# First mixer of a two-block transformer kernel: eight of twelve modulation blocks summed on GpSimd instead of TensorE

## The chip, the cores and the metric

One Trainium2 chip, one of its cores. The metric is the device time of one execution in microseconds (us), the median of the runs that are shown.

## What is computed

Two blocks, one after the other, on 256 tokens of width 1024 in fp32. The first block starts from a vector `c` of 1024 numbers that sets shifts, scales and gates:

```python
mod = jax.nn.silu(c) @ w_ada[l] + b_ada[l]                       # w_ada: 1024 x 6144
shift1, scale1, gate1, shift2, scale2, gate2 = jnp.split(mod, 6, axis=-1)
h = modulate(rms_norm(x, norm1_g[l]), shift1, scale1)
proj = h @ w_in[l]                                               # 1024 x 5120
q_sb, k_sb, v_sb, q_mb, k_mb, v_mb, g_sb, g_mb = jnp.split(proj, cuts, axis=-1)
o_sb, o_mb = stick_breaking_attention(...), moba_attention(...)
merged = sigmoid(g_sb) * (o_sb @ w_branch_sb[l]) + sigmoid(g_mb) * (o_mb @ w_branch_mb[l])
x = x + gate1[:, None, :] * (merged @ w_out[l])
h2 = modulate(rms_norm(x, norm2_g[l]), shift2, scale2)
y = moe_ffn(h2, ...)                                             # 64 experts, top 8
x = x + gate2[:, None, :] * y
```

The second block has a convolution, a low-rank attention, a cross attention to a memory and a second mixture of 16 experts. The change touches only `silu(c) @ w_ada`, which is cut into twelve blocks of 512 columns, called ada0 to ada11.

## The kernel before

The kernel is one program with an instruction list written by hand for each engine. All weights of the first mixer come through a ring of six places of 2 MB (`ring`, places of 128 partitions x 4096 fp32). `CHUNKS_A` (line 152) is the order in which SyncE (SP) loads them, all through line 581. A chunk of `w_in`, `w_branch` or `w_out` is split into two parts: ScalarE writes the rounded high part into the next place of the ring (`high`, line 799, four quarters of 128x1024), VectorE writes the rest over the chunk (`low_part`, line 1178, four quarters), and TensorE multiplies three times, high by high, high by low, low by high. Such a chunk takes two slots (`slots_of`, line 172), a modulation block takes one, as `WHOLE` says. Slot m lies in place m mod 6, and the chunk of slot m may be loaded when slot m-6 is given back: SP (line 595) and ScalarE before it writes a high part (line 793) wait for the count `used_a`, which TensorE raises at its first product behind the last use of a slot, or once that last use is done.

A modulation block on TensorE has two parts. `modulation(n, ...)` (line 2112) makes eight products of 128x32 with 512 columns, silu(c) against the block, into a bank of PSUM; ScalarE copies the bank to SBUF (`ada_copy`, the helper at line 776). `columns(n - 1)` (line 2100) then makes four products with one column each, which turn the row of 512 numbers into four columns of bank 7. `mod_full` counts these. VectorE waits for ten of them at line 1325, before it merges the two branches.

The order on TensorE: ada0 to ada3; in0, in1, in2, ada4, in3, in4, ada5, in5 (each in chunk about 11 us); then four steps p = 0 to 3, one for each pair of heads:

```python
zz{p}, ss{p}            # scores, lines 2219 to 2230
project in{6+p}_0       # line 2016; columns(5 + p); attend(p - 1), line 2211
half of in{6+p}_1       # line 2024
wait sb_rest; skip{p}   # lines 2243 to 2245
wait at_p_ready; pT{p}  # lines 2250 to 2252
half of in{6+p}_1; modulation(6 + p)
```

`sb_rest` comes from VectorE's line 1300, `at_p_ready` from its line 1306, behind the lines 1277 to 1305 of the same step. VectorE then makes quarters 0 and 1 of the low part of chunk 7+p, line 1318, and quarters 2 and 3, which the next step's in chunk needs. Behind the four steps come the branches (line 2268: three quarters of brs_0, `columns(9)`, attend(3), three of brs_1, then brm_0 and the rest), out0 to out3 (line 2016), the sums of squares (line 2059), ada10 and ada11 (`modulation` at lines 2302 and 2303), logit1 (line 2309) and the routing. `columns(10)` and `columns(11)` run in gate2, during the routing.

Behind the first mixer, the experts of the first mixture stream through the same ring: four fixed ones first, then those that the routing table names. GpSimd (POOL) does nothing but four constants at the start.

## Time and profile before

| | |
|---|---|
| median of 3 runs | 1531.04 us (1530.39 to 1534.06) |
| the profiled execution | 1528.67 us |
| its span, first to last instruction | 1526.9 us |
| first mixer up to logit1 | 0 to 247 us |
| routing | 247 to 269 us |
| first mixture of experts | 269 to 757 us |
| second mixer | 757 to 1086 us |
| second mixture of experts | 1086 to 1514 us |
| TensorE busy | 87% of the span |
| GpSimd busy | 0.2 us |

Busy time is counted for compute instructions. Start times are microseconds from the start of the span. "idle before" is the time that the engine stood still ahead of a group, with what released it behind the arrow.

### The profile page before, as it was taken

Reading aid. Unit: us, or ns where it says so; the run is one execution under the profiler, and the core shown is the slowest. Engines: PE = TensorE matmul, PEld = TensorE weight load, DVE = VectorE, ACT = ScalarE, POOL = GpSimd, SP = SyncE. Lnnn points to the kernel's source line nnn. Section 1 sums busy time; section 2 is a strip of 40 time slices with the busy share of each in tenths; the row PEclk is TensorE's granted clock in tenths of the full one; section 3 lists DMA queues with packets and bytes.
Section 4 is the critical chain, followed back from the end, with each engine's and each line's share of the span. In section 5 each row is a group of like instructions: output and inputs, shape, how many; then the busy total and the mean of one; then the engine's idle time right before and its main releaser. Section 6 shows DMA issues by size and latency. Waiting matters only on the chain.

```text
span 1526.9 us, 26211 instructions
## 1 busy us (share of the span) xinstructions
PE 1321.8 (87%) x11250; PEld 935.0 (61%) x11250; DVE 540.3 (35%) x1185; ACT 405.9 (27%) x630; POOL 0.2 (0%) x4
## 2 busy tenths in 40 slices
PE   6999998999999999999799999999876567566656
PEld 3888897666766765565588999999623213223222
DVE  3546665434233222322474775753301001001001
ACT  3557743111111111111264346452201000000001
POOL 0000000000000000000000000000000000000000
PEclk9999999999999999999999999999989869779787
DMA  9864659799999999999933344747999999999995
GB/s 398 304 267 169 275 208 393 307 408 388 425 423 422 428 424 424 424 421 420 409 129 143 139 161 166 279 165 296 391 427 428 427 428 429 428 428 428 429 428 231
DMA packets 46365, 523.58 MB, mean 343 GB/s; under 512 B 5273, under 2 KB 6841, under 8 KB 8761
## 3 DMA queue, kind: packets, MB, share of 16 engines
q1 hardware_dynamic: 44784, 519.16, 82.3%
q10 hardware_dynamic: 1480, 2.96, 0.6%
q8 instruction: 78, 1.28, 0.3%
q14 instruction: 23, 0.18, 0.0%
HBM read 520.85 MB, written 1.24 MB: 342 GB/s over the span
## 4 chain that ended last, share of the span: by engine, by line
PE 63%; DMA 31%; DVE 3%; ACT 1%; issue 1%; SPq 0%; ACTq 0%; DVEq 0%
PE psum L2016 17%; DMA arena<-in_w_exp_up_dram 14%; PE psum L2480 10%; DMA arena<-in_w_exp_down_dram 9%; PE psum L2580 5%; DMA ring<-in_w_gate_up_e_dram 4%; PE psum L2413 3%; PE psum L2996 3%; PE psum L2402 3%; DMA ring<-in_w_down_e_dram 2%; PE psum L2024 2%; PE psum L2268 2%; PE psum L2030 1%; PE psum L2835 1%; PE psum L2451 1%; DMA ring<-in_w_ada_dram 1%
## 5 line engine op out<-in xcount | busy, mean ns | idle before, releaser
L2016 PE MATMUL psum<-arena_r,ring_r 128*128 128x256 f32 x2176 | 272.5, 281 | 3.5 <-DVE arena_r L1185 3.1
L2016 PEld LDWEIGHTS psum<-arena_r,ring_r 128*128 128x128 f32 x2176 | 261.3, 188 | 8.7 <-issue 4.9
L2480 PE MATMUL psum<-ring,arena 128*32 128x256 f32 (+1 forms) x2304 | 184.2, 391 | 10.0 <-DMA ring<-in_w_gate_up_e_dram 9.3
L1178 DVE TENSOR_TENSOR ring_r<-ring,ring_r 128x1024 fp32r<-128x1024 f32 x140 | 163.0, 1219 | 59.9 <-ACT ring_r L799 59.2
L2480 PEld LDWEIGHTS psum<-ring,arena 128*32 128x32 f32 (+1 forms) x2304 | 111.1, 123 | 75.2 <-issue 16.5
L2996 PE MATMUL psum<-ring,arena 128*32 128x256 f32 x1408 | 103.2, 448 | 52.2 <-DMA ring<-in_w_exp_gate_dram 28.3
L799 ACT ACTIVATE ring_r<-ring 128x1024 fp32r<-128x1024 f32 x140 | 137.4, 1050 | 18.3 <-DMA ring<-in_w_out_dram 5.2
L2996 PEld LDWEIGHTS psum<-ring,arena 128*32 128x32 f32 x1408 | 48.8, 125 | 99.6 <-DMA ring<-in_w_exp_gate_dram 32.3
L3013 PE MATMUL psum<-ring,arena 128*32 128x512 f32 x384 | 67.2, 835 | 41.3 <-DMA ring<-in_w_exp_down_dram 37.5
L1951 DVE TENSOR_TENSOR arena<-arena,psum 128x256 f32<-128x256 f32 x16 | 6.7, 422 | 237.0 <-ACT arena L1137 237.0
L2580 PE MATMUL psum<-ring,arena 128*32 128x512 f32 (+1 forms) x544 | 87.6, 597 | 2.7 <-DMA ring<-in_w_down_e_dram 1.8
L1134 ACT ACTIVATE arena<-psum 128x512 f32<-128x512 f32 x16 | 9.6, 597 | 257.4 <-PE psum L2996 257.4
L776 ACT ACTIVATE arena<-psum 128x512 f32<-128x512 f32 (+3 forms) x76 | 43.6, 580 | 125.0 <-PE psum L2746 27.4
L3013 PEld LDWEIGHTS psum<-ring,arena 128*32 128x32 f32 x384 | 12.2, 132 | 91.6 <-DMA ring<-in_w_exp_down_dram 63.9
L2996 PE MATMUL psum<-arena 128*32 128x256 f32 x576 | 44.6, 466 | 26.9 <-DMA arena<-in_w_exp_up_dram 26.9
L938 ACT ACTIVATE arena<-psum 128x512 f32<-128x512 f32 x25 | 14.9, 598 | 195.3 <-PE psum L2480 195.3
L1586 DVE SCALAR_TENSOR_TENSOR arena_r<-psum,small,arena_r 128x512 fp32r<-128x512 f32 x25 | 18.8, 750 | 134.8 <-ACT arena_r L960 134.8
L2402 PE MATMUL psum<-arena_r 128*128 128x256 f32 x400 | 61.3, 291 | 3.2 <-DVE arena_r L1590 3.2
L1561 DVE COPY arena<-psum 128x384 f32<-128x384 f32 (+1 forms) x60 | 35.1, 585 | 78.5 <-PE psum L2413 76.8
L2402 PEld LDWEIGHTS psum<-arena_r 128*128 128x128 f32 x400 | 52.8, 190 | 10.8 <-issue 5.8
L2413 PE MATMUL psum<-arena_r 128*128 128x384 f32 (+1 forms) x304 | 55.7, 323 | 0.8 <-DVE arena_r L1467 0.8
L2580 PEld LDWEIGHTS psum<-ring,arena 128*32 128x32 f32 (+1 forms) x544 | 24.4, 120 | 52.2 <-issue 49.3
(425 smaller groups left out, 1524.4 us busy)
## 6 DMA issues: line engine op xcount, KB each, us to landing
ring<-in_w_gate_up_e_dram SPq DMA_DIRECT2D x56, 2048.0 KB, 16.8
ring<-in_w_down_e_dram SPq DMA_DIRECT2D x60, 1024.0 KB, 14.9
ring<-in_w_exp_gate_dram SPq DMA_DIRECT2D x29, 2048.0 KB, 35.2
ring<-in_w_exp_down_dram SPq DMA_DIRECT2D x24, 2048.0 KB, 35.8
ring<-in_w_in_dram SPq DMA_DIRECT2D x20, 2048.0 KB, 8.7
ring<-in_w_exp_up_dram SPq DMA_DIRECT2D x15, 2048.0 KB, 35.7
arena<-in_w_exp_up_dram SPq DMA_DIRECT2D x15, 2048.0 KB, 36.2
ring<-in_w_ada_dram SPq DMA_DIRECT2D x12, 2048.0 KB, 12.5
```

The lines of the kernel that those rows point to most:

```text
L776: frees(A(dst, src, ACT.Copy), name)
L799: A(hi, whole, ACT.Copy).then_inc(w_high, 1)
L1178: V.tensor_tensor(lo, whole, hi.bitcast(F32), ALU.subtract).then_inc(w_low, 1)
L1561: V.tensor_copy(dst, src).then_inc(g_copied, 1)
L2016: ins = product(lambda a_, b_, k, first, last: mm(ps[:, t * T:(t + 1) * T], a_[:, k, c], b_[:, k, :], start=first, stop=last), w, x, None ...
L2024: return product(lambda a_, b_, k, first, last: mm(ps[:, t * T:(t + 1) * T], a_[:, k, c], b_[:, k, :], start=first, stop=last, skip_group_ ...
L2402: ins = mm(acc(m), y[:, m * P:(m + 1) * P], PT1[j], start=(opens and m % 2 == 0 and y is y_hi), stop=False, skip_group_check=True)
L2413: ins = mm(psum[:, 4 + 3 * (n % 2), k * width:(k + 1) * width], h[:, t, kk * P:(kk + 1) * P], Pg1[:, t, c0:c0 + width], start=(t == 0 and ...
L2480: ins = mm(psum[c, 5, 256 * r:256 * r + 256], xg1[:, k, P * j + width * e:P * j + width * (e + 1)], w[:, k, :], start=(k == 0), stop=(k == ...
L2580: ins = mm(psum[width * b:width * (b + 1), 4 + 3 * half, :], hidden(b, e, k), dn[e][:, k, half * 512:(half + 1) * 512], start=(k == 0), st ...
L2996: ins = mm(psum[32 * q:32 * q + 32, b, g], xg[:, kk, CAP2 * e:CAP2 * (e + 1)], w[k][:, 256 * q:256 * (q + 1)], start=(kk == 0), stop=(kk = ...
L3013: ins = mm(psum[32 * e:32 * e + 32, 5 + 2 * half, :], aT2[e][:, k, :], w(e)[:, half * 512:(half + 1) * 512], start=(k == 0), stop=(k == KT ...
```

## The change

The eight products of ada4 to ada11 leave TensorE, and ScalarE's eight copies go with them. GpSimd gets a program of its own: when a block has landed, it multiplies each of its eight 128x512 parts by the number of silu(c) that belongs to the partition, in place, then adds halves (2048 columns, then 1024, then 512) until one row of 512 per partition is left. TensorE's four one-column products now sum over all 128 partitions, with ones in place of the selecting column. Each of the three adds waits for the one before it, the last one also for `mod_full`.

The blocks move in the ring's order: ada6 to ada9 one place of the order ahead, and ada10 and ada11 from behind `w_out` to behind in9. The slots of the eight blocks are given back by GpSimd (`mod_rows`), all others by TensorE (`used_a`). `columns(4)` stands behind in4, `columns(5)` to `columns(9)` where they stood. The load of `w_up_sh` moves behind the four fixed experts.

```diff
-ADA_BEHIND = {2: (4,), 4: (5,), 6: (6,), 7: (7,), 8: (8,), 9: (9,)}
-ADA_PAIR = 6
+ADA_BEHIND = {2: (4,), 4: (5,), 5: (6,), 6: (7,), 7: (8,), 8: (9,), 9: (10, 11)}
...
-CHUNKS_A += [("w_branch_sb", 0, 1024, 4), ("w_branch_mb", 0, 1024, 4), ("w_out", 0, 512, 8), ("w_out", 512, 512, 8),
-             ("w_ada", 512 * (ADA - 2), 512, 8), ("w_ada", 512 * (ADA - 1), 512, 8)]
+CHUNKS_A += [("w_branch_sb", 0, 1024, 4), ("w_branch_mb", 0, 1024, 4), ("w_out", 0, 512, 8), ("w_out", 512, 512, 8)]
...
-NU = NA
+GP_SLOTS = [SLOT_A[IN_ADA[_j]] for _j in range(ADA_FIRST, ADA)]
+NU = NA - len(GP_SLOTS)
...
-        csil = buf(6, 8, 256)
+        csil = mod[:, 40:48]
...
+        summed_rows = ada_rows + [buf(12, 512, 512 * _i) for _i in (1, 2, 3, 1, 2, 3)]
...
+        def given_back(eng, m):
+
+            if m in GP_SLOTS:
+                eng.wait_ge(mod_rows, GP_SLOTS.index(m) + 1)
+            else:
+                eng.wait_ge(used_a, sum(s not in GP_SLOTS for s in range(m + 1)))
...
-                    sp.wait_ge(used_a, SLOT_A[n] - RING + 1)
+                    given_back(sp, SLOT_A[n] - RING)
...
-            sp.wait_ge(mod_full, ADA - 2)
-            sp.dma_start(up_sh, a["w_up_sh"].rearrange("p (k f) -> p k f", k=KT)).then_inc(up_sh_in, 16)
             pair(0, (E1 - 4, E1 - 3))
             pair(3, (E1 - 2, E1 - 1))
+            full(sp, "gate2")
+            sp.dma_start(up_sh, a["w_up_sh"].rearrange("p (k f) -> p k f", k=KT)).then_inc(up_sh_in, 16)
...
-                for n in ADA_BEHIND.get(c, ()):
-                    ada_copy(n)
...
-                if p:
-                    ada_copy(ADA_PAIR - 1 + p)
...
-            copy_out("ada10", late_rows[0])
-            copy_out("ada11", late_rows[1])
...
+        @block.gpsimd
+        def _(gp):
+            G = nc.gpsimd
+            gp.wait_ge(csil_ready, 1)
+            steps = 0
+            for n in range(ADA_FIRST, ADA):
+                arrived(gp, ("a", IN_ADA[n]))
+                w = ring[:, SLOT_A[IN_ADA[n]] % RING, :].rearrange("p (k c) -> p k c", k=KT)
+                for k in range(KT):
+                    ins = G.tensor_scalar(w[:, k, :], w[:, k, :], csil[:, k:k + 1], None, ALU.mult)
+                ins.then_inc(gp_step, 1)
+                for half in (4, 2):
+                    steps += 1
+                    gp.wait_ge(gp_step, steps)
+                    G.tensor_tensor(w[:, 0:half, :], w[:, 0:half, :], w[:, half:2 * half, :], ALU.add).then_inc(gp_step, 1)
+                steps += 1
+                gp.wait_ge(gp_step, steps)
+                gp.wait_ge(mod_full, n - 1 if n < ADA_FIRST + 2 else n - 2)
+                if n == ADA_FIRST + 2:
+                    full(gp, "ms0")
+                G.tensor_tensor(summed_rows[n - ADA_FIRST], w[:, 0, :], w[:, 1, :], ALU.add).then_inc(mod_rows, 1)
...
-                evacuated(pe, f"ada{n}")
+                if n < ADA_FIRST:
+                    evacuated(pe, f"ada{n}")
+                    rows, over = ada_rows[n % 2], sel_col
+                else:
+                    pe.wait_ge(mod_rows, n - ADA_FIRST + 1)
+                    rows, over = summed_rows[n - ADA_FIRST], ones[:, 0:1]
...
-                for i, n in enumerate(ADA_BEHIND.get(c, ())):
-                    modulation(n, IN_A[c] + 1 + i, held)
-                    held = None
+                if c == 4:
+                    pe.wait_ge(mod_ready, 2)
+                    columns(ADA_FIRST).then_inc(mod_full, 1)
...
                     if p and i == 0:
-                        ins.then_inc(used_a, 1)
+                        ins.then_inc(used_a, 2)
...
-                modulation(ADA_PAIR + p, IN_A[6 + p] + 1, (used_a, 2))
...
-            modulation(ADA - 2, n0 + 14)
-            modulation(ADA - 1, n0 + 15, gives=(used_a, 1))
```

Three places show how the instructions move. SP's loads in the first mixer, from in5 on, in the kernel before (every load waits for TensorE's count):

```order
L581 DMA ring<-in_w_in_dram 128x4096 [waits chunks_used_a] x2
L581 DMA ring<-in_w_ada_dram 128x4096 [waits chunks_used_a]
L581 DMA ring<-in_w_in_dram 128x4096 [waits chunks_used_a]
L581 DMA ring<-in_w_ada_dram 128x4096 [waits chunks_used_a]
L581 DMA ring<-in_w_in_dram 128x4096 [waits chunks_used_a]
```

The same stretch of SP's loads in the changed kernel:

```order
L590 DMA ring<-in_w_in_dram 128x4096 [waits modulation_rows_summed]
L590 DMA ring<-in_w_ada_dram 128x4096 [waits chunks_used_a]
L590 DMA ring<-in_w_in_dram 128x4096 [waits chunks_used_a]
L590 DMA ring<-in_w_ada_dram 128x4096 [waits modulation_rows_summed]
L590 DMA ring<-in_w_in_dram 128x4096 [waits chunks_used_a]
L590 DMA ring<-in_w_ada_dram 128x4096 [waits modulation_rows_summed]
```

Every modulation block but two, in5 and out0 now stand behind GpSimd's count; in5 waits for ada4, ada7 for ada5, and so on.

TensorE from the end of one pair step into the next, in the kernel before (L2024 is the last half of the in chunk, L2112 the modulation, L2219 the next scores):

```order
L2024 MATMUL psum<-arena_r,ring_r 128x256 x24
L2112 MATMUL psum<-ring,items 32x512 x8
L2219 MATMUL psum<-arena 128x256 x2
L2223 MATMUL psum<-arena 128x128 x2
L2228 MATMUL psum<-arena 128x128 x2
L2230 MATMUL psum<-arena 128x256 x2
L2016 MATMUL psum<-arena_r,ring_r 128x256 x48
```

and in the changed kernel:

```order
L2052 MATMUL psum<-arena_r,ring_r 128x256 x24
L2237 MATMUL psum<-arena 128x256 x2
L2241 MATMUL psum<-arena 128x128 x2
L2246 MATMUL psum<-arena 128x128 x2
L2248 MATMUL psum<-arena 128x256 x2
L2044 MATMUL psum<-arena_r,ring_r 128x256 x48
```

The eight products between two steps are gone; the in chunk follows sooner on the step before.

GpSimd's list for one block in the changed kernel (it stands there eight times):

```order
L1172 TENSOR_SCALAR ring<-ring,mod 128x512 x8
L1177 TENSOR_TENSOR ring<-ring 128x2048
L1177 TENSOR_TENSOR ring<-ring 128x1024
L1183 TENSOR_TENSOR arena<-ring 128x512
```

Before, GpSimd had no such instruction.

## Rows read from the trace of the kernel before

**Rows 1.** The page: busy time of each engine.

```profile
PE 1321.8 (87%) x11250; PEld 935.0 (61%) x11250; DVE 540.3 (35%) x1185; ACT 405.9 (27%) x630; POOL 0.2 (0%) x4
```

**Rows 2.** Windows: length, busy PE, PEld, DVE, ACT, POOL, granted clock, DMA share, GB/s.

```profile
108.00:190.00 82.00, 80.13 (x686) 69.93 (x685) 55.16 (x81) 59.72 (x94) 0.00 (x0) 1.00 0.56 221
450.00:550.00 100.00, 98.73 (x812) 67.58 (x812) 31.59 (x96) 13.19 (x22) 0.00 (x0) 1.00 1.01 423
```

**Rows 3.** Timeline of TensorE: start, length, line, instructions, idle before.

```profile
68.41 1.92 PE L2112 MATMUL psum<-ring,items 128*32 128x512 f32 x16
70.77 11.44 PE L2016 MATMUL psum<-arena_r,ring_r 128*128 128x256 f32 x96 [0.44 <-PE psum L2112]
...
111.79 5.88 PE L2016 MATMUL psum<-arena_r,ring_r 128*128 128x256 f32 x48
...
126.51 1.92 PE L2112 MATMUL psum<-ring,items 128*32 128x512 f32 x16
128.36 0.70 PE L2219 MATMUL psum<-arena 64*128 64x256 f32 x4
...
188.03 2.37 PE L2268 MATMUL psum<-arena_r,ring_r 128*128 128x256 f32 x18 [0.78 <-ACT arena L776]
...
192.56 20.75 PE L2268 MATMUL psum<-arena_r,ring_r 128*128 128x256 f32 x174
```

**Rows 4.** Timeline of all engines from ada10 to the first logits.

```profile
242.03 3.64 PE L2112 MATMUL psum<-ring,items 128*32 128x512 f32 x32
246.53 3.30 ACT L913 ACTIVATE arena<-arena,mod 128x256 f32<-128x256 f32 x8 [1.74 <-DVE arena L1214]
247.19 3.34 PE L2309 MATMUL psum<-arena 128*64 128x256 f32 x16 [1.52 <-ACT arena L913]
```

**Rows 5.** Windows around a stretch in which TensorE stands still.

```profile
757.00:759.00 2.00, 0.16 (x2) 0.15 (x2) 1.93 (x4) 2.00 (x4) 0.00 (x0) 1.00 1.00 426
761.00:763.00 2.00, 2.00 (x12) 2.00 (x11) 2.00 (x5) 1.52 (x3) 0.00 (x0) 0.50 0.64 239
```

**Rows 6.** DMA, 160 to 216 us: the branch loads, median us from issue to landing.

```profile
ring<-in_w_branch_sb_dram SPq DMA_DIRECT2D x1, 2048.0 KB, 7.5
ring<-in_w_branch_mb_dram SPq DMA_DIRECT2D x1, 2048.0 KB, 12.4
```

**Rows 7.** Groups of VectorE by form, 46 to 200 us: busy us, mean ns.

```profile
L1178 DVE TENSOR_TENSOR ring_r<-ring,ring_r 128x1024 fp32r<-128x1024 f32 x40 | 46.8, 1221 | 26.2 <-ACT ring_r L799 26.1
L1306 DVE TENSOR_SCALAR arena<-arena,small 128x256 f32<-128x256 f32 x8 | 2.8, 346 | 0.0
L1285 DVE SCALAR_TENSOR_TENSOR arena<-psum,arena 128x512 f32<-128x512 f32 x4 | 2.7, 680 | 0.0
L1305 DVE TENSOR_SCALAR arena<-arena,small 128x128 f32<-128x128 f32 x8 | 2.3, 283 | 0.1
```

**Rows 8.** Timeline of SP and ScalarE: the load of ada4, the high part of out0.

```profile
46.23 0.33 SPq L581 DMA_DIRECT2D ring<-in_w_ada_dram  x1
...
203.67 3.90 ACT L799 ACTIVATE ring_r<-ring 128x1024 fp32r<-128x1024 f32 x4 [3.28 <-DVE arena L1338]
```

**Rows 9.** One pair step (p = 1) on VectorE and TensorE, in order of time.

```profile
136.09 0.69 DVE L1300 TENSOR_TENSOR arena<-arena,constants 128x512 f32<-128x512 f32 x1
138.09 0.34 DVE L1306 TENSOR_SCALAR arena<-arena,small 128x256 f32<-128x256 f32 x1
140.81 0.59 PE L2243 MATMUL psum<-arena,constants 128*128 128x256 f32 x2
142.56 0.27 PE L2250 MATMUL psum<-constants,arena 128*128 128x128 f32 x1
145.27 2.36 DVE L1178 TENSOR_TENSOR ring_r<-ring,ring_r 128x1024 fp32r<-128x1024 f32 x2 [1.55 <-ACT ring_r L799]
149.48 5.87 PE L2016 MATMUL psum<-arena_r,ring_r 128*128 128x256 f32 x48
```

**Rows 10.** VectorE ahead of the first pair step.

```profile
101.12 3.26 DVE L1255 SCALAR_TENSOR_TENSOR arena<-arena,vectors 128x256 f32<-128x256 f32 x8 [5.61 <-ACT arena L823]
```

More of the change, by code:

```diff
@@ L199 @@
 for _c in range(6):
-    JOBS += [f"in{_c}_{_j}" for _j in range(2)] + {3: ["ms0"], 4: ["sum0"]}.get(_c, []) + [f"ada{_j}" for _j in ADA_BEHIND.get(_c, ())]
+    JOBS += [f"in{_c}_{_j}" for _j in range(2)] + {3: ["ms0"], 4: ["sum0"]}.get(_c, [])
 for _p in range(PAIRS):
-    JOBS += [f"zz{_p}", f"ss{_p}", f"in{6 + _p}_0"] + ([f"av{_p - 1}"] if _p else []) + [f"in{6 + _p}_1", f"skip{_p}", f"pT{_p}", f"ada{ADA_PAIR + _p}"]
+    JOBS += [f"zz{_p}", f"ss{_p}", f"in{6 + _p}_0"] + ([f"av{_p - 1}"] if _p else []) + [f"in{6 + _p}_1", f"skip{_p}", f"pT{_p}"]
 JOBS += ["brs_0", f"av{PAIRS - 1}", "brs_1", "brm_0", "brm_1", "brs_2", "brm_2", "brs_3", "brm_3"]
-JOBS += ["out0", "out1", "out2", "ms2", "out3", "ada10", "ada11", "logit1"]
+JOBS += ["out0", "out1", "out2", "ms2", "out3", "logit1"]
 JOBS += ["hN0", "route1", "hN1", "hN2", "hN3", "gate2", "shg", "rank1", "count1", "tabT", "start1", "itemR", "itemW", "eidx"]
@@ L230 @@
         continue
-    while (_name == "logit1" and _next % BANKS != 6) or (_name == "cq" and _next % BANKS != 4) or (_name == "ms7" and _next % BANKS <= 3):
+    while (_name == "brs_2" and _next % BANKS != 2) or (_name == "logit1" and _next % BANKS != 6) or (_name == "cq" and _next % BANKS != 4) or (_name == "ms7" and _next % BANKS <= 3):
         _next += 1
@@ L2092, in idle_products, with columns, modulation @@
                     mm(ps[:, 0:T], ones, cst[:, 0:T], start=True, stop=True)
-            def columns(n, place=None, rows=None, gives=None):
-                evacuated(pe, f"ada{n}")
+            def columns(n, place=None):
+                if n < ADA_FIRST:
+                    evacuated(pe, f"ada{n}")
+                    rows, over = ada_rows[n % 2], sel_col
+                else:
+                    pe.wait_ge(mod_rows, n - ADA_FIRST + 1)
+                    rows, over = summed_rows[n - ADA_FIRST], ones[:, 0:1]
                 place = psum[:, 7, 4 * ADA_ORDER[n]:4 * ADA_ORDER[n] + 4] if place is None else place
-                rows = (pair_rows if n >= ADA_PAIR else ada_rows)[n % 2] if rows is None else rows
                 for b in range(4):
-                    ins = mm(place[:, b:b + 1], rows[:, b * P:(b + 1) * P], sel_col, start=True, stop=True)
-                    if gives is not None and b == 0:
-                        ins.then_inc(*gives)
+                    ins = mm(place[:, b:b + 1], rows[:, b * P:(b + 1) * P], over, start=True, stop=True)
                 return ins
-            def modulation(n, place, gives=None):
+            def modulation(n, place):
                 w = chunk_a(place, 512)
@@ L2113, in modulation @@
                                  start=(k == 0), stop=(k == 1))
[L2114 to L2115 removed]
                 done(ins, f"ada{n}")
[L2117 to L2126 removed]
+                full(pe, f"ada{n}")
+                used(used_a, 1)
             def norm_sums(name, sqb, ready):
@@ L2146, in _ @@
             columns(ADA_FIRST - 1).then_inc(mod_full, 1)
-            n0 = IN_A[9] - 8
             def project_by_halves(w):
@@ L2273, in branch @@
                     done(ins, name)
-            ws = chunk("a", n0 + 10, whole=False)
-            branch("brs_0", ws, 0, 0, range(3), SPLIT_AT[("a", n0 + 10)], gives=(used_a, 1))
+            ws = chunk("a", IN_BRANCH["s"], whole=False)
+            branch("brs_0", ws, 0, 0, range(3), SPLIT_AT[("a", IN_BRANCH["s"])], gives=(used_a, 2))
             columns(ADA - 3).then_inc(mod_full, 1)
@@ L2279, in _ @@
             branch("brs_1", ws, 0, 2, range(3))
-            wm = chunk("a", n0 + 11, whole=False)
+            wm = chunk("a", IN_BRANCH["m"], whole=False)
             evacuated(pe, f"skip{PAIRS - 1}")
-            branch("brm_0", wm, 4, 0, range(3), SPLIT_AT[("a", n0 + 11)])
-            branch("brs_0", ws, 0, 0, (3,), SPLIT_AT[("a", n0 + 10)])
-            branch("brm_0", wm, 4, 0, (3,), SPLIT_AT[("a", n0 + 11)])
+            branch("brm_0", wm, 4, 0, range(3), SPLIT_AT[("a", IN_BRANCH["m"])])
+            branch("brs_0", ws, 0, 0, (3,), SPLIT_AT[("a", IN_BRANCH["s"])])
+            branch("brm_0", wm, 4, 0, (3,), SPLIT_AT[("a", IN_BRANCH["m"])])
             branch("brs_1", ws, 0, 2, (3,))
```

37 lines of the change are left out of this document (15 added, 22 removed).

## The prediction

> **What bounds the kernel now.** I read the page first: TensorE is busy 87% of the span, VectorE 35%, ScalarE 27%, and GpSimd 0.2 us [rows 1]. The windows then tell the stages apart [rows 2]. In the first mixer TensorE works 80.1 of 82 us, while the DMA engines have a share of 0.56: TensorE bounds, and what leaves its list there is time, unless something else is late. Around 450 to 550 us the DMA share is 1.01 and TensorE is busy 98.7 of 100: the experts run at the speed of the loads. But those loads start when TensorE gives ring places back, so an earlier mixer starts that stretch earlier by as much, and a later one later. I carry every microsecond of the mixer to the end one for one.
>
> **What the change takes away.** The timeline of TensorE prices it [rows 3]. From the start of ada4 to the start of in3 it is 70.77 - 68.41 = 2.36 us. ada5 to ada9 each cost the distance from their start to the next work, 128.36 - 126.51 = 1.85 us; five make 9.25 us. The wait of 0.78 us ahead of 188.03 is for ScalarE's copy of ada9 and goes with it. Together 12.4 us. The one-column products stay. ada10 and ada11 are 3.64 us, yet worth nothing: from 242 us on ScalarE and VectorE make the norm and the modulated input, and TensorE's logits start at 247.19, released by ScalarE, 1.5 us after ada11 is over [rows 4]. Without them TensorE stands still for those 5 us. Elsewhere a stop has cost clock: from 757 to 759 TensorE worked 0.16 us, the granted clock was still 1.00, and in 761 to 763 it was 0.50, which is 1.2 of 2.4 GHz [rows 5]. The logits and transposes behind the gap could run at that level for some of the routing. They are half paced by ScalarE, so I put this at 1 us, bounds 0 and 3.
>
> ScalarE's eight copies, off the path, cost nothing and give nothing. w_up_sh goes behind the fixed experts, whose loads gain the place of ada10 and ada11: nothing either way, since the share in the mixer leaves room [rows 2].
>
> **What the new order of the ring costs.** w_branch_mb was loaded into the place of ada8, which came back at the start of the last pair step, and took 12.4 us to land beside w_branch_sb, which took 7.5 [rows 6]. Now it needs in9's place, which comes back only at the first product of brs_0. That product moves from 188.03 to about 175.6. The load lands 7.5 us after it, at 183.5 with the issue; one quarter on ScalarE (3.90 us for four) and one on VectorE (1.22) [rows 7, 8] make the first quarter ready at 185.9, the others follow at 1.2 us each, and the fourth, behind the copy of av3 on ScalarE, at about 189.7. TensorE wants it earlier: in the timeline brm_0 starts 18 products of 0.119 us after 192.56, at 194.7 [rows 3], so at 182.3 now. It ends its first pass some 5.6 us late. This cost doesn't depend on GpSimd.
>
> Up to here: -12.4 + 5.6 + 1 = **-5.8 us**.
>
> **What GpSimd costs.** No row shows a GpSimd instruction of this kind; the nearest are VectorE's [rows 7]. From 283 ns for 128 columns and 346 for 256, both from SBUF to SBUF, a product of 512 is about 0.47 us on VectorE, 0.49 ns a column. The plain pace is that of 680 ns for 512 and 1221 for 1024, 1.06 ns a column. The adds of 2048, 1024 and 512 come to 2.3, 1.22 and 0.68 by it. So a block is 8 x 0.47 + 4.2 = 8.0 us if GpSimd has VectorE's best pace, and 2 x (8 x 0.68 + 4.2) = 19.3 at half its plain one. I take 12 us, nearer to the plain pace (9.6) because these are the same operations; 11 instructions, 1.09 us in the mean. That alone is hidden: ada4, issued at 46.23, has landed by about 57; the eighth sum must be there for the high part of out0, at 203.67 before and some 7 us sooner now [rows 8], and 139 us over eight is 17.4 us a block.
>
> What is not hidden is the company of VectorE. The two prices of a product above (0.49 ns a column against 1.06) show that VectorE draws on a second path to SBUF where it can. I assume that this path is GpSimd's too, and that an instruction of VectorE which wants it waits for the GpSimd instruction in progress. No row of this trace speaks for or against, for GpSimd never runs beside VectorE here. The Trainium skill, SBUF — State Buffer, section "Who interferes with whom", states it outright: a VectorE instruction with two SBUF inputs contends with a GpSimd instruction that reads SBUF, and the one that comes second blocks until the first is done. By that page the sum is the one that follows, without it -5.8.
>
> With 12 us of work in a step that shrinks to 17.8 us, GpSimd is busy 0.67 of the time, and a VectorE instruction loses 0.67 x 1.09 = 0.73 us. In a pair step there are eleven of them: lines 1292, 1296, 1300, four of 1305 and 1306, four of 1178.
> - Up to the skip products three lose 2.2 us. Line 1300 ended at 136.78, TensorE came at 140.81: 4.0 us of slack [rows 9]. Nothing.
> - Up to pT seven lose 5.1 us, slack 142.56 - 138.43 = 4.1: **1.0 us**.
> - The last two quarters of the next chunk's low part ended at 147.63, and TensorE wanted them at 149.48. These 1.85 us are just what the missing modulation takes away, so their delay of 1.5 us counts in full: **1.5 us**.
>
> 2.5 us in each of three steps is 7.5. Ahead of the first step stand eight of line 1255 and the four quarters of in6. The eight start at 101.12 [rows 10], now 4.2 us earlier at 97, and take 1.14 each instead of 0.41: to 106.1. Four quarters at 1.95 bring it to 113.9, where TensorE wants them at 111.79 - 4.2 = 107.6 [rows 3]: 6.3 us. Two quarters in the branches: 1.5 us. Sum 15.3, net of -5.8: **+9.5 us**.
>
> With 8 us a block the same working gives 0.33 us an instruction, 5 us in all, net -1. With 16 us it gives 1.3 us each: 7.7 a step, 13.4 ahead of them, 2.6 in the branches, 39 in all, net +33. Against the profiled execution of 1528.67 us this is 1538.2, and since the median of the runs shown lies 2.4 us above it, 1540.6 us; the forecast's own range is 1530 to 1565.
>
> The Trainium skill has the one price of GpSimd that I know: GPSIMD Engine Reference, section 3.1, gives 4497 ns for an add of 2048 columns against 2293 on VectorE. By it the adds take 8.3 us instead of the 6 or so in my 12, a block some 14, and the sum would be about +20.
>
> **Rivals.**
> 1. *The two engines don't meet.* The splits run at 1.22 us as before, GpSimd is hidden below 17.4 us a block, and what is left is -5.8: 1525.2 us, faster. For it speaks that nothing in the trace shows a shared path; against it the second path that the product prices show. It decides as soon as the delay of a VectorE instruction is under about 0.35 us, where the stalls fall below 5.8. Chance 0.34, of which 0.25 is faster by over 0.3% (4.6 us, about what a measurement of this kernel can tell from no change) and 0.09 within.
> 2. *GpSimd is simply too slow.* Beyond 17.4 us a block the eighth sum is late for out0, whatever VectorE does; at 19.3 it comes 8 x 1.9 = 15 us late, net +9, and the blocks behind it in the ring (in5 behind ada4, in7 behind ada7) begin to drag: 1540 to 1560. Chance 0.10.
> 3. *They meet, but GpSimd gives way.* VectorE's eleven instructions are some 8.5 us of a step, which leaves GpSimd 9.3 for its 12: it falls 2.7 us behind in each of four steps and a few more in the projections, well inside the 8 x 5.4 us that it has to spare. VectorE then waits only at the first instruction of a row, for the rest of what GpSimd has begun, in all 3 to 8 us: 1528 to 1533. Chance 0.10: 0.03 faster, 0.05 within, 0.02 slower.
>
> The forecast has the other 0.46: 0.39 slower by over 0.3%, 0.07 within. Sums: 0.28 faster, 0.21 within 0.3%, 0.51 slower. The range reaches from rival 1 with its bounds, 1523, to the forecast with 16 us a block, 1566.
>
> **What would show it.** In the profile of the changed kernel: line 1178's successor stays at 1.22 us in the mean if rival 1 holds, or is well above it; the GpSimd rows sum to 12 us a block, or over 17. TensorE idles ahead of the in chunks of the pair steps, released by VectorE's low part, in the forecast, and nowhere but at brm_0 in rival 1. An idle stretch of about 5 us ahead of logit1 with a lower granted clock behind it, and w_branch_mb issued at the first product of brs_0, belong to every case. I am wrong at the root if the mixer changes by one amount and the whole by another, that is, if the experts don't pass the shift on.

## The result, and the profile after

The changed kernel takes 1585.18 us (median of 4 runs, 1583.62 to 1585.81), the kernel before 1530.72 us in the runs beside it (4 runs, 1526.07 to 1534.06): a ratio of 1.0359, 95% interval 1.0342 to 1.0376. Slower by 54.5 us, where I had forecast 9.5, and 19 us past the end of my range. The profiled execution has a span of 1584.0 us against 1526.9 before.

The page of the changed kernel, busy time of each engine and the first row of the chain that ended last:

```profile
PE 1322.8 (84%) x11122; PEld 948.3 (60%) x11122; DVE 577.5 (36%) x1185; ACT 401.5 (25%) x622; POOL 200.1 (13%) x92
...
PE 50%; DMA 30%; POOL 13%; DVE 4%; ACT 2%; issue 1%; SPq 0%; POOLq 0%; ACTq 0%; DVEq 0%
```

TensorE has lost its 128 products (11250 before) and is no less busy: its mean granted clock over the span is 0.923, against 0.941 before. The first version below, with the same 11122 products and hardly any work on GpSimd, is busy 1307.4 us; so some 15 us of TensorE's busy time go to the lower clock behind its waits, and belong to the delay. GpSimd is new with 200.1 us, and it stands in the chain with 13% of the span, about as much. I had 96 us in mind for it (8 x 12). Its groups by form (busy us, mean ns, idle before):

```profile
L1172 POOL TENSOR_SCALAR ring<-ring,mod 128x512 f32<-128x512 f32 x64 | 125.5, 1977 | 54.9 <-DMA ring<-in_w_ada_dram 54.9
L1177 POOL TENSOR_TENSOR ring<-ring 128x2048 f32<-128x2048 f32 x8 | 37.7, 4711 | 0.7
L1177 POOL TENSOR_TENSOR ring<-ring 128x1024 f32<-128x1024 f32 x8 | 22.9, 2856 | 0.6
L1183 POOL TENSOR_TENSOR arena<-ring 128x512 f32<-128x512 f32 x8 | 14.0, 1751 | 0.6
```

A product takes 1977 ns in the mean, where I had 0.68 us as the dearer bound by VectorE's rows [rows 7]. How much of that is GpSimd's own shows in the last block of its timeline, since VectorE has no instruction between 235.3 and 258.3 us (start, us, line, instructions):

```profile
208.66 18.57 POOL L1172 TENSOR_SCALAR ring<-ring,mod 128x512 f32<-128x512 f32 x8
227.31 7.44 POOL L1177 TENSOR_TENSOR ring<-ring 128x2048 f32<-128x2048 f32 x2
234.83 1.61 POOL L1183 TENSOR_TENSOR arena<-ring 128x512 f32<-128x512 f32 x1
236.43 12.34 POOL L1172 TENSOR_SCALAR ring<-ring,mod 128x512 f32<-128x512 f32 x8
248.85 6.91 POOL L1177 TENSOR_TENSOR ring<-ring 128x2048 f32<-128x2048 f32 x2
255.83 1.26 POOL L1183 TENSOR_TENSOR arena<-ring 128x512 f32<-128x512 f32 x1
```

The last block takes 257.09 - 236.43 = 20.7 us by itself: eight products of 1.54 us, adds of 6.91 together and 1.26. The one before it took 27.8. The eight blocks run back to back from 55.27 to 257.09 us, 25.2 us each: behind its first product GpSimd stands still for 1.9 us in all (the last column above, where 54.9 us lie ahead of that product). So no load, no ring place and no other engine sets the end of the eighth sum, but GpSimd's own pace. My sum had 12, and my upper bound was 19.3.

Who waits for that? The waits of ScalarE and of SP's queue between 50 and 320 us (waited for: us, times, longest):

```profile
ACT ring_r L811 <- POOL arena L1183: 38.5, 2, 27.7
```

```profile
SPq L590 <- POOL arena L1183: 122.3, 6, 25.6
```

SP waits six times, 122.3 us, for a place that GpSimd holds, and ScalarE waits 27.7 us for the eighth sum, which must be there before the high part of out0 is written (line 799 before, 811 now). TensorE on its side, same columns:

```profile
PE psum L2044 <- DVE arena_r L1213: 23.8, 2, 20.9
PE psum L2044 <- DVE ring_r L1206: 8.6, 4, 4.4
PE psum L2237 <- DVE arena L1346: 8.3, 3, 4.4
PE psum L2285 <- DVE ring_r L1206: 7.0, 2, 5.8
```

The timeline of TensorE says where: these are the starts that answer to rows 3 and 4, with the idle time before them in brackets.

```profile
211.34 1.94 PE L2285 MATMUL psum<-arena_r,ring_r 128*128 128x256 f32 x6 [5.78 <-DVE ring_r L1206]
...
263.79 2.90 PE L2044 MATMUL psum<-arena_r,ring_r 128*128 128x256 f32 x12 [20.89 <-DVE arena_r L1213]
269.56 17.84 PE L2044 MATMUL psum<-arena_r,ring_r 128*128 128x256 f32 x132 [2.87 <-DVE arena_r L1213]
...
302.64 2.79 PE L2324 MATMUL psum<-arena 128*64 128x256 f32 x11 [5.09 <-ACT arena L921]
```

| start of | before, us | after, us | later by |
|---|---|---|---|
| first pair step | 110.28 | 108.74 | -1.5 |
| second pair step | 128.36 | 133.26 | 4.9 |
| fourth pair step | 167.57 | 182.05 | 14.5 |
| brs_0 | 188.03 | 211.34 | 23.3 |
| out0 | 213.15 | 263.79 | 50.6 |
| logit1 | 247.19 | 302.64 | 55.5 |

From logit1 to the end it is 1281.4 us now and 1279.7 before: the experts pass the shift on, as predicted. Everything happens before logit1, so **the start of logit1 is the measure** in what follows, beside the time. It serves for versions that leave work out too, as nothing before it depends on the values, while the routing behind it does.

Each version has one trace, and the traces differ before GpSimd has anything to do. The load of ada4, issued at 46.23 us in the kernel before [rows 8], is issued here in the change and in the version with short adds below:

```profile
47.06 0.33 SPq L590 DMA_DIRECT2D ring<-in_w_ada_dram  x1
```

```profile
50.65 0.33 SPq L590 DMA_DIRECT2D ring<-in_w_ada_dram  x1
```

The versions spread from 46.03 to 50.83 us, and none of this is GpSimd's work, which starts some 8 us later. Where a few microseconds decide, I therefore count the start of logit1 **from that issue**: 200.96 us before, 255.58 us in the change, 54.6 later, as the time is.

VectorE was held as well, and the row shows it plainly. The eight instructions of line 1283 (line 1255 before, [rows 10]) read and write SBUF:

```profile
98.07 11.23 DVE L1283 SCALAR_TENSOR_TENSOR arena<-arena,vectors 128x256 f32<-128x256 f32 x8 [2.27 <-ACT arena L835]
```

3.26 us before, 11.23 now. The splits of line 1206 (line 1178 before) take 1781 ns in the mean between 46 and 260 us, against 1221 [rows 7], the longest 5.6 us. So two suspects remain: GpSimd's own chain of blocks, and VectorE blocked by GpSimd.

### The profile page after: what moved, and what is told of

Read it like the earlier page. It is cut to its first block, busy times and chain, and to the rows that moved or that the text cites. A ratio compares the mean times of both kernels' runs of the same rounds, so it can differ in the third digit from the quotient of the medians.

```text
span 1584.0 us, 26036 instructions
## 1 busy us (share of the span) xinstructions
PE 1322.8 (84%) x11122; PEld 948.3 (60%) x11122; DVE 577.5 (36%) x1185; ACT 401.5 (25%) x622; POOL 200.1 (13%) x92
## 3 DMA queue, kind: packets, MB, share of 16 engines
q10 hardware_dynamic: 1480, 2.96, 0.6%
q8 instruction: 77, 1.26, 0.3%
## 4 chain that ended last, share of the span: by engine, by line
PE 50%; DMA 30%; POOL 13%; DVE 4%; ACT 2%; issue 1%; SPq 0%; POOLq 0%; ACTq 0%; DVEq 0%
DMA arena<-in_w_exp_up_dram 14%; PE psum L2044 13%; DMA arena<-in_w_exp_down_dram 9%; PE psum L2495 9%; POOL ring L1172 8%; PE psum L2595 5%; DMA ring<-in_w_gate_up_e_dram 4%; POOL ring L1177 4%; PE psum L2428 3%; PE psum L3011 3%; PE psum L2417 2%; DMA ring<-in_w_down_e_dram 2%; PE psum L2850 1%; PE psum L2466 1%; PE psum L2182 1%; PE psum L2464 1%
## 5 line engine op out<-in xcount | busy, mean ns | idle before, releaser
L2044 PE MATMUL psum<-arena_r,ring_r 128*128 128x256 f32 x2176 | 283.4, 287 | 34.0 <-DVE arena_r L1213 25.3
L2044 PEld LDWEIGHTS psum<-arena_r,ring_r 128*128 128x128 f32 x2176 | 272.0, 195 | 39.7 <-issue 23.6
L1206 DVE TENSOR_TENSOR ring_r<-ring,ring_r 128x1024 fp32r<-128x1024 f32 x140 | 186.7, 1388 | 102.1 <-ACT ring_r L811 100.8
L811 ACT ACTIVATE ring_r<-ring 128x1024 fp32r<-128x1024 f32 x140 | 137.5, 1050 | 77.0 <-POOL arena L1183 38.5
L2495 PEld LDWEIGHTS psum<-ring,arena 128*32 128x32 f32 (+1 forms) x2304 | 109.7, 121 | 71.9 <-issue 13.4
L1172 POOL TENSOR_SCALAR ring<-ring,mod 128x512 f32<-128x512 f32 x64 | 125.5, 1977 | 54.9 <-DMA ring<-in_w_ada_dram 54.9
L788 ACT ACTIVATE arena<-psum 128x512 f32<-128x512 f32 (+3 forms) x68 | 38.6, 577 | 105.3 <-PE psum L2761 27.4
L1177 POOL TENSOR_TENSOR ring<-ring 128x2048 f32<-128x2048 f32 (+1 forms) x16 | 60.5, 3784 | 1.3
```

The source lines that it names most:

```text
L788: frees(A(dst, src, ACT.Copy), name)
L811: A(hi, whole, ACT.Copy).then_inc(w_high, 1)
L1172: ins = G.tensor_scalar(w[:, k, :], w[:, k, :], csil[:, k:k + 1], None, ALU.mult)
L1177: G.tensor_tensor(w[:, 0:half, :], w[:, 0:half, :], w[:, half:2 * half, :], ALU.add).then_inc(gp_step, 1)
L1206: V.tensor_tensor(lo, whole, hi.bitcast(F32), ALU.subtract).then_inc(w_low, 1)
L2044: ins = product(lambda a_, b_, k, first, last: mm(ps[:, t * T:(t + 1) * T], a_[:, k, c], b_[:, k, :], start=first, stop=last), w, x, None ...
```

## The experiments

Theory A: the chain. Eight blocks one behind the other end too late for the ring and for out0. Theory B: the company. VectorE's low parts are late because GpSimd's instructions hold it. The first four kernels ran before any of them was known.

**The work left out.** The change with only the last add of each block:

```diff
-                for k in range(KT):
-                    ins = G.tensor_scalar(w[:, k, :], w[:, k, :], csil[:, k:k + 1], None, ALU.mult)
-                ins.then_inc(gp_step, 1)
-                for half in (4, 2):
-                    steps += 1
-                    gp.wait_ge(gp_step, steps)
-                    G.tensor_tensor(w[:, 0:half, :], w[:, 0:half, :], w[:, half:2 * half, :], ALU.add).then_inc(gp_step, 1)
...
```

> The changed kernel with GpSimd's eight products and first two adds of every block left out: one add of 512 columns a block stays, so the modulation of ada4 to ada11 is not computed. Theory A (the chain of GpSimd's blocks, 25.2 us each from 55.3 to 257.1 us, carries the first mixer): the chain is gone, the mixer is shorter than before by the 5.8 us of the forecast's first sum, 1525 us. Theory B (VectorE held up by GpSimd's reads is the main cost): also gone with so few reads, 1525 us. If w_branch_mb behind in9 costs other than 5.6 us, or a gap ahead of logit1 more than 1 us, the difference shows here.

Measured: 1529.02 us, ratio 0.9991 (0.9981 to 1.0). logit1 at 246.37 us, 1.3 us earlier than before by the count from ada4's issue, not the 6.8 that the forecast's first two terms give (-12.4 + 5.6). So all of the change's loss is GpSimd's work; and what the change saves on TensorE is nearly all lost with hardly any work on GpSimd. SP's timeline of this version shows one reason:

```profile
145.68 16.86 SPq L590 DMA_DIRECT2D ring<-in_w_ada_dram  x2
162.58 1.51 SPq L590 DMA_DIRECT2D ring<-in_w_branch_sb_dram  x1
179.51 0.33 SPq L590 DMA_DIRECT2D ring<-in_w_branch_mb_dram  x1
```

w_branch_sb goes out behind ada10 and ada11 and w_branch_mb only at 179.51, against 168.30 before.

**Company alone, beside the kernel before.** 66 products that read constants and write an idle place, then 180 memsets, each waiting for the one before it:

```diff
+            for _i in range(66):
+                if _i:
+                    gp.wait_ge(gp_done, _i)
+                G.tensor_scalar(idle_place, cst[:, 0:512], cst[:, 640:641], None, ALU.mult).then_inc(gp_done, 1)
```

> The kernel before, with 66 GpSimd products of 128x512 from about 83 us on, from constants into a place that nobody reads: only their company is added, no wait but that of the load of w_up_sh behind the last. Theory B: line 1178 and lines 1283 to 1334 of VectorE get slower while they run, 1.8 instead of 1.22 us a quarter, TensorE waits in the pair steps, 1540 to 1550 us. Theory A: company is nearly free, below 3 us, 1531 to 1534 us. If both hold, the result here is B's share of the 54 us.

> As the run with reads, but 180 memsets of 128x512, which write and do not read SBUF. Both theories, if the shared thing is the read path: VectorE stays at 1.22 us, 1531 us. If writes hold VectorE up as well, it shows as in the run with reads.

Measured: 1532.43 us with the products, ratio 1.0016 (0.9999 to 1.0033), and 1529.24 with the memsets, 1.0001 (0.9987 to 1.0014). The products slowed VectorE's splits from 1221 to 1300 ns only. It was rather GpSimd that gave way:

```profile
L1168 POOL TENSOR_SCALAR arena<-constants 128x512 f32<-128x512 f32 x66 | 129.4, 1960 | 89.0 <-PE psum L2062 82.9
```

1960 ns beside VectorE, about 1.55 alone. 129 us of such company cost some 2 us (logit1 2.2 later), so **one-operand products hardly hurt**, and are slowed by VectorE themselves. The memsets left the splits at 1221 ns; among the rows of VectorE only its TENSOR_SCALAR from SBUF to SBUF, 283 and 346 ns before [rows 7], went to some 520, with the products to some 535.

**One long product for eight.** 

```diff
-                for k in range(KT):
-                    ins = G.tensor_scalar(w[:, k, :], w[:, k, :], csil[:, k:k + 1], None, ALU.mult)
-                ins.then_inc(gp_step, 1)
+                c3 = csil.unsqueeze(2).to_broadcast([P, KT, 512])
+                G.tensor_tensor(w[:, :, :], w[:, :, :], c3, ALU.mult).then_inc(gp_step, 1)
```

> The changed kernel with the eight products of a block made as one two-operand product of 4096 columns (silu(c) repeated along the columns). The adds run at 2.3 ns a column alone, the one-operand products at 3.04, so a block should take 9.4 + 8.2 = 17.6 us alone instead of 20.7, and some 22 in company instead of 25.2. Theory A: out0 moves by eight times that, 25 us, and the time is about 1560 us. Theory B: the same number of reads, one long instruction instead of eight: VectorE waits up to 9 us at a time, the time stays at 1580 us or more.

Measured: 1596.83 us, ratio 1.0431 (1.0413 to 1.0448), worse than the change though a block has less work in it. The product takes 7416 ns, and VectorE's timeline (start, us, line, instructions) stands still beside it:

```profile
106.69 28.85 DVE L1282 SCALAR_TENSOR_TENSOR arena<-arena,vectors 128x256 f32<-128x256 f32 x8 [2.28 <-ACT arena L835]
135.46 8.03 DVE L1205 TENSOR_TENSOR ring_r<-ring,ring_r 128x1024 fp32r<-128x1024 f32 x1
```

The eight instructions of 3.26 us now take 28.85, about one for each GpSimd instruction of two operands. TensorE waits 48.6 us for VectorE's low parts. So theory B is real for two-operand instructions, and it is dear where they are long; this version came out in its range. GpSimd here waits too, 10.6 us for TensorE and 38.5 us for loads behind the first, so its chain no longer sets the end. Which one rules in the change is still open.

**Products only, adds only, and a chain that reads nothing.** From the change one part is taken out each time; in the third, five memsets of 4096 columns stand in for products and adds.

```diff
+                for i in range(5):
...
+                    G.memset(w[:, :, :], 0.0).then_inc(gp_step, 1)
```

> The changed kernel without the first two adds of each block (the modulation is wrong: two of eight products are summed). GpSimd has 8 products of 1.56 us alone (1.96 in company) and a last add of 1.3 to 1.75 us a block: 13.8 to 17.5 us instead of 20.7 to 25.2. Theory A (the time past 1529 is GpSimd's chain: eight blocks back to back hold the ring and out0, which begins when a block takes over 17.4 us): 1530 to 1540 us. Theory B (the time is VectorE held up by GpSimd's instructions, in proportion to GpSimd's busy time): two thirds of the 56 us between the light version and the change, 1560 to 1570 us. VectorE's 1024-column subtractions: under 1500 ns mean under A, 1600 and more under B.

> The changed kernel without the eight products of each block (the modulation is wrong: unweighted rows are summed). GpSimd has the three adds alone, 4.7 + 2.9 + 1.8 = 9.3 us a block, far below 17.4. Theory A (chain): no block is late, 1529 to 1532 us, as the light version with one add. Theory B (VectorE held up): the adds, with two operands read, are what holds VectorE, and 1540 to 1565 us, with single subtractions of up to 5.6 us.

> The changed kernel with five memsets of 128x4096 in the place of the products and the first two adds of each block (the modulation is wrong: zeros are summed). A memset reads nothing and left VectorE's subtractions at 1221 ns; by 530 ns for 512 columns five take 19 to 21 us, a block 20.5 to 22.5 us. Theory A (chain): the ring and out0 are held as in the change, by eight blocks in 165 to 180 us; the time 1555 to 1570 us, over 1529 by eight times what a block takes over 17.4. Theory B (VectorE held up): 1529 to 1535 us. VectorE's subtractions near 1221 ns under both.

**The ring's order.** The light version with the two last modulation blocks behind w_out, as in the kernel before:

```diff
-ADA_BEHIND = {2: (4,), 4: (5,), 5: (6,), 6: (7,), 7: (8,), 8: (9,), 9: (10, 11)}
+ADA_BEHIND = {2: (4,), 4: (5,), 5: (6,), 6: (7,), 7: (8,), 8: (9,)}
...
-CHUNKS_A += [("w_branch_sb", 0, 1024, 4), ("w_branch_mb", 0, 1024, 4), ("w_out", 0, 512, 8), ("w_out", 512, 512, 8)]
+CHUNKS_A += [("w_branch_sb", 0, 1024, 4), ("w_branch_mb", 0, 1024, 4), ("w_out", 0, 512, 8), ("w_out", 512, 512, 8),
+             ("w_ada", 512 * (ADA - 2), 512, 8), ("w_ada", 512 * (ADA - 1), 512, 8)]
```

> The light version (one add a block, the modulation wrong) with the two last modulation blocks loaded where the kernel before loads them, behind both halves of w_out, so that brs and brm come two ring places earlier. If the light version gave its 12 us back because brs and brm came late by the ring's order: out0 starts 6 to 10 us earlier (from 212.3 to 202 to 206 us) and the time is 1519 to 1525 us. If TensorE's lower clock or the DMA's rate takes it: 1527 to 1530 us.

Measured: 1529.52 us with the products (ratio 0.9993, 0.9976 to 1.001), 1572.04 with the adds (1.0275, 1.0246 to 1.0303), 1544.23 with the memsets (1.0082, 1.0054 to 1.0111), and 1520.11 for the light version in the old order (0.9928, 0.9907 to 0.9948). The adds' time can't be set beside the others: without the products other experts are chosen, TensorE has 11336 products instead of 11122, and 1309 us pass behind logit1 instead of 1281. By logit1, counted from ada4's issue, the adds cost 15.4 us over the light version, the products 2.9. So the adds cost that much by their company alone, in blocks of 9.9 us that the ring has time for: theory A had expected nothing there. The memsets cost 13.2, less than A's 26 to 41 and more than B's 0 to 6, with the splits at 1218 ns; but the softmax's TENSOR_SCALAR took 2.5 to 2.9 us beside them, so this was no clean chain. The order alone is worth 7.9 us, as was expected: logit1 at 237.83, with w_branch_mb issued at 161.47.

**A cleaner chain, short adds, short everything, and the order with the full work.**

```diff
+                for i in range(36):
...
+                    ins = G.memset(w[:, i % 8, :], 0.0)
```

```diff
-                    G.tensor_tensor(w[:, 0:half, :], w[:, 0:half, :], w[:, half:2 * half, :], ALU.add).then_inc(gp_step, 1)
+                    for k in range(half):
+                        ins = G.tensor_tensor(w[:, k, :], w[:, k, :], w[:, half + k, :], ALU.add)
+                    ins.then_inc(gp_step, 1)
```

The third has these short adds, `G.tensor_tensor(w[:, k, :], w[:, k, :], csil[:, k:k + 1].to_broadcast([P, 512]), ALU.mult)` as its products, and the old order; the fourth is the change with the old order.

> The changed kernel with 36 memsets of 128x512 a block in the place of products and first two adds (the modulation is wrong: zeros are summed). GpSimd is busy 36 x 0.53 + 1.3 = 20.4 us a block, what the change's block takes alone, in writes of at most 0.53 us. Theory A (the chain of blocks alone makes the delay): logit1 at 246.4 (light version) + 8 x (20.4 - 17.4) = 24, so 268 to 274 us instead of 302.6, and a time of 1547 to 1556. Theory B (the delay comes by VectorE): logit1 at 246 to 252 us, 1529 to 1534. VectorE's 1024-column subtractions at 1221 ns, its two TENSOR_SCALAR of the softmax step (2.5 to 2.9 us beside memsets of 3.54 us) back at 0.5 to 0.6 us.

> The changed kernel, the same sums, with the two first adds cut into pieces of 512 columns: six GpSimd instructions of 1.3 to 1.7 us for two of 4.7 and 2.9 us. GpSimd's block takes 21 to 26 us as before. If VectorE is held for the length of one long add (single subtractions of up to 5.6 us): their longest falls to 3 us, logit1 comes 8 to 15 us earlier, 1570 to 1577 us. If the chain of blocks alone sets the end: 1583 to 1590 us.

> The same sums in pieces of 512 columns throughout, the products as TENSOR_TENSOR against a broadcast column (0.88 us a piece by the 7.02 us of the one long product, against 1.56), and the two last blocks loaded behind w_out as in the kernel before. A block takes 8 x 0.9 + 7 x 1.3 = 16.3 us alone, under the 17.4 that the ring allows. Chain theory: no block late, 1520 to 1530 us. If two-operand reads hold VectorE in short pieces as in long ones: 1540 to 1560 us.

> The changed kernel with only the ring's order restored: the two last modulation blocks are loaded behind both halves of w_out. Six blocks instead of eight stand between the loads and out0. By the chain: out0's weights come two blocks earlier (2 x 25 us), logit1 at 262 to 275 us instead of 302.6, and 1543 to 1557 us. If the delay is VectorE's, the same work holds it and 1570 to 1585 us.

Measured: 1539.87 us (1.0056, 1.0036 to 1.0075), 1590.82 (1.0384, 1.0361 to 1.0406), 1552.22 (1.014, 1.011 to 1.017) and 1572.55 (1.0273, 1.0253 to 1.0294). The short adds are the telling miss: VectorE's splits came down from 1956 to 1611 ns in the mean (50 to 210 us), the longest from 5.6 to 2.3 us, and yet logit1 came 5.3 us later than in the change (from ada4's issue; the medians differ by 5.6 us, the ratios by less, and their intervals touch), because the eight blocks took 5.1 us longer. That is theory A, against B. The short memsets fell between the two theories, as the five long ones had (1539.87 us, for 1547 to 1556 or 1529 to 1534): their block took 19.0 us instead of 20.4. The table puts the versions with the change's order together; the end of the eighth sum is read from GpSimd's timeline, whose last rows are, for the short memsets, then for the short adds:

```profile
189.81 2.30 POOL L1183 TENSOR_TENSOR arena<-ring 128x512 f32<-128x512 f32 x1
...
209.49 1.29 POOL L1183 TENSOR_TENSOR arena<-ring 128x512 f32<-128x512 f32 x1
```

```profile
243.31 1.29 POOL L1185 TENSOR_TENSOR arena<-ring 128x512 f32<-128x512 f32 x1
...
264.58 1.26 POOL L1185 TENSOR_TENSOR arena<-ring 128x512 f32<-128x512 f32 x1
```

| version, in the change's order | eighth sum ends, us | logit1, us | between | logit1 from ada4's issue |
|---|---|---|---|---|
| light | 171.4 | 246.37 | 75.0 | 199.7 |
| adds only | 190.1 | 261.98 | 71.9 | 215.1 |
| products only | 199.5 | 250.02 | 50.5 | 202.6 |
| short memsets | 210.8 | 255.71 | 44.9 | 209.6 |
| five memsets | 217.7 | 263.71 | 46.0 | 212.9 |
| one long product | 246.5 | 317.93 | 71.5 | 267.3 |
| **the change** | 257.1 | 302.64 | 45.5 | 255.6 |
| short adds | 265.8 | 311.50 | 45.7 | 260.9 |

Four versions with quite different company for VectorE stand at 45 to 46 us: there the eighth sum decides, microsecond for microsecond, and the change is one of them (the other three give 45.5 without it). The floor is the light version's 199.7 us from ada4's issue, so a sum later than 199.7 - 45.5 = 154.2 counts in full; the chain starts 8.2 us after that issue in the change, which leaves (154.2 - 8.2) / 8 = 18.2 us a block. The other rows lie above 46, and are held elsewhere: the light version and the products by neither of the two, the adds alone and the one long product by VectorE.

Where the old order takes the last two blocks out of out0's way, 25 us are won against the change at logit1 (277.75 us), and with shorter work in it 43 (259.6). Both stay above the light version's 237.83, by 38.6 and 21.2 us from ada4's issue: SP still waits 98.3 us for blocks in the former, and its splits take 2036 ns.

The times won are smaller, 12.6 and 33 us, for here logit1 isn't the whole measure. From logit1 to the end it takes 1291.4 and 1291.7 us, where the light version in the old order takes 1278.8: the last two blocks now run beside the norm and the routing. In the full-work version with the old order TensorE waits 9.1 us for the eighth sum in gate2:

```profile
295.01 1.87 PE L2133 MATMUL psum<-constants,arena 128*128 128x1 f32 x8 [9.11 <-POOL arena L1184]
```

Both times also lie in the ranges expected for theory B, not in the chain's. For the short work the chain's range rested on blocks of 16.3 us; its last block took 18.2 us alone (a product of 512 columns 1.18 us instead of 0.9), and the first six 23.1 us each. So the chain carries the change, but it isn't all that eight blocks on GpSimd cost: take it away from out0, and the full work still costs some 40 us over the kernel before.

**Company where no block is late.** Two more runs tell what company costs by itself, with correct sums and few blocks. They are the kernel before, with only ada4 and ada5 on GpSimd, first in the change's instructions, then in pieces of 512 columns:

```diff
+BY_GP = (4, 5)
...
+            for n in BY_GP:
```

> The kernel before with only ada4 and ada5 summed by GpSimd, in the change's instructions, and the ring's order untouched. TensorE saves 2.4 + 0.8 + 1.9 = 5.1 us, and GpSimd is busy from 55 to 107 us, ahead of the pair steps. Chain theory (nothing waits for a block, since the next chunk in its slot has slack): logit1 at 242 to 244 us instead of 247.2 and 1526 to 1528 us. If company costs 2 us a block as adds alone did (15.6 us for eight): logit1 at 246 to 249 us, 1529 to 1533. If ada5's block, which ends near 107 us, holds in8's or in9's load: later still, 1535 and more.

> The same two blocks in pieces of 512 columns (products as TENSOR_TENSOR against a broadcast column): 23 us a block in company. If the length of a GpSimd instruction is what holds VectorE: 1 to 2 us less than e13_two_blocks. If any read of two operands does: 1 to 3 us more. Both between 1524 and 1535 us.

Measured: 1532.81 us, ratio 1.0018 (1.0009 to 1.0027), and 1526.81 us, ratio **0.9979** (0.997 to 0.9988), each over 11 runs. logit1 at 252.99 and 245.97 us, from ada4's issue 3.4 us later and 2.7 us earlier than before. TensorE's timeline of the first of them, at the first product of in6, and the windows around it (columns as in rows 2):

```profile
114.95 8.49 PE L2045 MATMUL psum<-arena_r,ring_r 128*128 128x256 f32 x48 [4.91 <-DVE ring_r L1207]
```

```profile
110.00:134.00 24.00, 19.09 (x139) 17.53 (x138) 16.99 (x23) 12.23 (x20) 0.00 (x0) 0.86 0.40 167
```

The first pair step came 4.2 us earlier from ada4's issue (1.8 us on the clock of the trace), the whole saving of ada4 and ada5. Then TensorE waited 4.9 us for in6's low part, since line 1284 before it (line 1255 of the kernel before) had taken 10.8 us for 3.3 beside the adds of ada5. The in chunk behind the wait ran 8.49 us for 5.88, at a mean granted clock of 0.86 in this window, which was 1.00 before: another 2.6. -4.2 + 4.9 + 2.6 = 3.3 us, which is all of the delay. In short pieces the in chunk starts like this:

```profile
110.39 5.92 PE L2047 MATMUL psum<-arena_r,ring_r 128*128 128x256 f32 x48 [1.37 <-DVE ring_r L1209]
```

The same eight take 5.3 us (725 ns in the mean), the wait is 1.4, the clock stays at 1.00, and the version is the first that beats the kernel before with nothing left out, if by 3 us only. I had expected 1 to 2 us between the two, and it is 6: one wait and the clock behind it. Products and adds changed together here, so which of them did it isn't shown.

## Why the prediction was wrong, step by step

- **(1) TensorE's 12.4 us.** Right in its rows, three quarters there. With the old order and hardly any company brs_0 starts at 178.47 for 188.03, 9.6 us earlier (9.4 from ada4's issue). The rest is lost at the first pair step: it waits 2.96 us for ScalarE's copy instead of 1.10, and the step shrinks by 0.3 us instead of 1.85, as its 48 products behind the wait take 6.77 us for 5.88, at a mean granted clock of 0.86. ada10 and ada11 were indeed worth nothing, since the idle stretch ahead of logit1 is 5.09 us, as forecast. The lower clock behind it is there too (0.50 from 303 to 306 us in the change), but the 1 us put on it isn't: the light version takes 1278.4 us from logit1 to the end, 1279.7 before.
- **(2) The ring's order, 5.6 us.** Right in its mechanism, too small: 7.9 us at logit1. I had only w_branch_mb late. w_branch_sb stands behind ada10 and ada11 as well, at 162.58 instead of 144.94. In the change w_branch_mb went out at 211.93 us, just behind the first product of brs_0 (211.34), as forecast.
- **(3) A block of 12 us, at most 19.3: the step that failed.** It was bounded from VectorE's rows by what one instruction moves. GpSimd's product took 1.54 us alone, over twice the plain price of 0.68 and above its double, and a block 20.7. The adds were no surprise: 8.2 us alone together, for 8.4 in the dearer bound. And no length of a block had in it that VectorE slows GpSimd: 25.2 us in company. The forecast let only VectorE pay. Rival 3 did let GpSimd fall behind, but with 12 us of work, for which there was room.
- **(4) The limit of 17.4 us a block**, which decides when the eighth sum is late, was good: the runs show 18.2. Put into it, the measured block gives 8 x (25.2 - 18.2) = 56 us over the light version, and logit1 is 55.9 later from ada4's issue. An estimate from these rows: 20 of them are GpSimd's own 20.7 us, 36 are what company adds to it.
- **(5) VectorE's 15.3 us.** The mechanism, that a VectorE instruction waits for the GpSimd instruction in progress, is there, and on no row plainer than on line 1283. But I gave every GpSimd instruction the same mean length. I also charged each wait with the whole of it (0.67 x 1.09 us), where an instruction that comes at any moment meets half of it on average; no run tells which is nearer. Products hardly hold VectorE (2.9 us for all eight blocks), adds do (15.4, as much as the forecast's 15.3, but from other instructions), a long product most. The Trainium skill, SBUF — State Buffer, section "Who interferes with whom", names two-input VectorE instructions as those that contend; the splits and line 1283 are such. Beside the adds they agree (11.23 us for 3.26), and beside the memsets, which read nothing, too (splits at 1221 ns). Beside the one-operand products they don't: these read SBUF as well, for 1.98 us each, and the splits lose only some 80 to 144 ns in the mean. In the change the delays lie beside the chain, and hardly add to it.

So it was **rival 2**, with a chance of 0.10 and a price of 1540 to 1560, since its block ended at 19.3 us. Its mechanism, the eighth sum late for out0 and the ring dragging behind, is what the trace shows. Nor did I price that the two mechanisms feed each other: company lengthens the block, and the block is what counts.

What stays open: why GpSimd's products slow down from 1.54 to 1.98 us beside VectorE and hardly hold its splits in return, and how much of the 38.6 us in the old order is company and how much is the ring. A version that keeps the company and gives the blocks places outside the ring would tell, and wasn't tried.

## What to carry to other kernels

Price an engine that has no row in the trace by a range that starts at the others' figures and goes to several times them, and then ask at what length its chain becomes late; here the limit was known to 1 us, and the length only to a factor of two. Work that is moved to an idle engine is not off the path if its buffer is a place in a ring that others wait for: order the loads so that nothing urgent stands behind it. Cut GpSimd's two-operand instructions short where VectorE works beside them and GpSimd has time to spare: with two blocks that turned a loss of 3 us into a gain of 3, with eight blocks, where GpSimd's own chain decided, short adds cost 5 us more. And compare traces from a common event, not from their start.

## What the hardware showed unexpectedly

- A GpSimd product of 512 columns with one operand and a column of scalars took 1.54 us alone, 3.0 ns a column; an add of two operands 6.91 us for 3072 columns, 2.2 ns; a two-operand product against a broadcast column 7.0 us for 4096, 1.7 ns, and in pieces of 512 columns 1.18 us, 2.3 ns. The instruction with fewer operands is the slowest.
- A long two-operand GpSimd instruction holds VectorE's two-operand ones and is itself little slowed (7.4 us for 7.0), and VectorE gets about one instruction in between: 28.85 us for eight of 0.48. In pieces of 512 columns GpSimd pays as well: an add took 1.25 us alone and 1.90 beside VectorE in the version with two short blocks. The one-operand product goes from 1.54 to 1.98 us, with VectorE's splits at 1300 to 1365 ns for 1221; VectorE's TENSOR_SCALAR of 283 ns takes some 530 beside it.
- Memsets don't touch the splits, but hold VectorE's TENSOR_SCALAR of 283 ns from SBUF to SBUF: 521 ns where each memset of 530 ns waits for the one before it, 2178 where eight follow without a wait, although their mean is the same (531 ns). I had expected 0.5 to 0.6 us there.
- After a wait of 4.9 us TensorE ran a stretch at a lower granted clock (48 products in 8.49 us, 5.88 before), after one of 3.0 us a shorter one (6.77), after one of 1.4 us none (5.92).
